# Second attention of a two-block transformer kernel: scaled keys, a negated row maximum, and output halves added by GpSimd

## The reference

```python
def attention_mixer(q, k, v, q_g, k_g, ang_row, ang_col):      # 8 query heads of 64, 2 key heads, 1024 tokens
    q = axial_rope(rmsnorm(q, q_g), ang_row, ang_col)
    k = axial_rope(rmsnorm(k, k_g), ang_row, ang_col)
    ...
    scale = HEAD_DIM ** -0.5                                    # 0.125
    def block(qblk):                                            # 128 queries
        s = jnp.einsum('bqkgd,bskd->bkgqs', qblk, k).astype(jnp.float32) * scale
        p = jax.nn.softmax(s, axis=-1)
        return jnp.einsum('bkgqs,bskd->bqkgd', p.astype(v.dtype), v)
```

## Time and profile before

| | |
|---|---|
| median of 3 runs | 2304.12 us (2303.63 to 2305.65) |
| span of the profiled execution | 2307.9 us |
| busy in the span: PE, DVE, ACT, POOL | 2218.0, 1617.7, 1089.5, 795.6 us |
| second attention | from 1357.5 us (first scores) to 1557.3 us (last values) |
| mean granted TensorE clock | 0.989 of full speed |

### The profile page before, as it was taken

The page is one execution under the profiler, slowest core; times in us unless marked ns, Lnnn a source line. Parts: engine busy times, 40 slices in busy tenths (PEclk is TensorE's granted clock), DMA queues, the critical chain, the costliest instruction groups (busy, mean ns, idle before and its releaser), DMA issues. The chain is left out here.

```text
span 2307.9 us, 29073 instructions
## 1 busy us (share of the span) xinstructions
PE 2218.0 (96%) x10136; PEld 1787.9 (77%) x10136; DVE 1617.7 (70%) x2247; ACT 1089.5 (47%) x1877; POOL 795.6 (34%) x579
## 2 busy tenths in 40 slices
PE   6999998999899999999998999999999999999998
PEld 4778887686678888888876767767778888887887
DVE  6468447626999999985797379994575555556686
ACT  5232256735644444455445368882343333334533
POOL 1030024513533232342023626661274444433310
PEclk9999999999999999999999999999999999999999
DMA  9156622033133333289944230003422333339986
GB/s 348 56 174 212 203 85 64 26 128 115 45 111 101 105 101 110 81 296 394 335 165 139 72 101 19 23 5 110 145 69 98 107 101 106 101 119 320 354 277 228
DMA packets 282565, 331.82 MB, mean 144 GB/s; under 512 B 18281, under 2 KB 180409, under 8 KB 282049
## 3 DMA queue, kind: packets, MB, share of 16 engines
q1 hardware_dynamic: 279760, 322.57, 41.4%
q0 software_dynamic: 2208, 7.37, 0.9%
q10 hardware_dynamic: 465, 0.17, 0.0%
HBM read 251.11 MB, written 78.94 MB: 143 GB/s over the span
## 5 line engine op out<-in xcount | busy, mean ns | idle before, releaser
L2643 PE MATMUL ps<-sum_hi,whi 128*128 128x512 f32 x640 | 249.5, 390 | 1.0 <-DVE wlo L2809 0.7
L2645 PE MATMUL ps<-sum_hi,wlo 128*128 128x512 f32 x640 | 249.0, 389 | 0.0
L2644 PE MATMUL ps<-sum_lo,whi 128*128 128x512 f32 x640 | 249.0, 389 | 0.0
L2669 PE MATMUL ps<-sum_lo,whi 128*128 128x512 f32 x616 | 240.7, 391 | 2.0 <-ACT arena L2754 2.0
L2671 PE MATMUL ps<-sum_lo,wlo 128*128 128x512 f32 x616 | 239.7, 389 | 0.0
L2670 PE MATMUL ps<-sum_lo,whi 128*128 128x512 f32 x616 | 239.7, 389 | 0.0
L2643 PE MATMUL ps<-hhi,whi 128*128 128x512 f32 x480 | 188.3, 392 | 9.0 <-DVE cbuf L3324 3.3
L226 DVE TENSOR_TENSOR wlo<-raw,whi 128x1024 fp32r<-128x1024 f32 x56 | 78.4, 1406 | 159.6 <-ACT whi L221 159.5
L2644 PE MATMUL ps<-hlo,whi 128*128 128x512 f32 x480 | 188.2, 392 | 0.0
L2645 PE MATMUL ps<-hhi,wlo 128*128 128x512 f32 x480 | 188.0, 392 | 0.0
L1732 POOL TENSOR_TENSOR cbuf<-cbuf,attn_stats 128x1024 f32<-128x1024 f32 x80 | 151.5, 1894 | 94.0 <-DVE attn_stats L1993 94.0
(11 more groups left out here) (450 smaller groups left out, 5575.2 us busy)
## 6 DMA issues: line engine op xcount, KB each, us to landing
shared<-ffn_blocks SPq DMA_DIRECT2D x154, 256.0 KB, 5.1
lead_work<-in_w_down SPq DMA_DIRECT2D x105, 256.0 KB, 4.4
arena<-in_w_down SPq DMA_DIRECT2D x100, 256.0 KB, 4.1
raw<-in_w_up SPq DMA_DIRECT2D x36, 512.0 KB, 5.1
ffn_blocks<-chunk_work SPq DMA_DIRECT2D x66, 256.0 KB, 2.3
ffn_blocks<-lead_work SPq DMA_DIRECT2D x66, 256.0 KB, 2.3
raw<-in_w_in SPq DMA_DIRECT2D x32, 512.0 KB, 4.7
arena<-in_w_ada SPq DMA_DIRECT2D x32, 512.0 KB, 5.5
```

Of the source, the lines that this page charges most:

```text
L2643: nc.tensor.matmul(o, hi[:, ws], mhi, start=fresh and k == 0, stop=False, skip_group_check=True)
L2644: nc.tensor.matmul(o, hi[:, ws], mlo, start=False, stop=False, skip_group_check=True)
L2645: mm = nc.tensor.matmul(o, lo[:, ws], mhi, start=False, stop=(k == 3), skip_group_check=True)
L2669: nc.tensor.matmul(o, hi[:, ws], mhi, start=fresh, stop=False, skip_group_check=True)
```

## The change

Four things are edited, all for the second attention alone. The keys are multiplied by 0.125 when they are split into high and low part, so the scores come out scaled and the exponential has no scale. The maximum is written with its sign turned by the reduction itself, and the small multiplication (L1977) is gone. ACT copies both halves of a group's output from PSUM, into `otmp` and a new `osum`. The two additions (old L2010) move from DVE's list to POOL's, behind the scaling of the closing unit, with a wait for ACT's copies ahead of them and a wait for their own end behind them.

```diff
-            otmp = cbuf[:, 2, 0:512]
+            otmp, osum = cbuf[:, 2, 0:512], cbuf[:, 2, 512:1024]
...
                     nc.scalar.activation(khh[64 * r:64 * r + 64, g, pad:kn], ka[64 * g:64 * g + 64, :],
-                                         ACT.Copy).then_inc(S["keys"], 1)
+                                         ACT.Copy, scale=SC if full else 1.0).then_inc(S["keys"], 1)
...
+                    if full:
+                        ins = nc.vector.scalar_tensor_tensor(out=klo[0:64, g, pad:kn], in0=k_, scalar=SC, in1=hi,
+                                                             op0=ALU.mult, op1=ALU.subtract)
...
+                    def outputs(n, gr, g):
+
+                        pool.wait_ge(S["out_copy"], gr.val(add=1))
+                        for half in range(2):
+                            o_, t_ = (v[0:64, :].rearrange("p (j s t) -> p j s t", s=2, t=P)[:, :, half, :] for v in (osum, otmp))
+                            ins = nc.gpsimd.tensor_tensor(qa[64 * half:64 * half + 64, 2 * g:2 * g + 2, tokens(n)],
+                                                          o_, t_, ALU.add)
+                        ins.then_inc(S["out"], 1)
+                        pool.wait_ge(S["out"], gr.val(add=1))
...
+                            gr = gr_closed(n, e)
+                            if gr is not None and full:
+                                outputs(n if e >= units else n + (-1), gr, 1 - e // units)
...
                     if full:
+                        outputs(At(NB - 1), group(At(NB - 1), per_n - 1), 1)
                         lead.pool_last(pool)
...
-                            nc.scalar.activation(prob[sl], up[sl][:, :], ACT.Exp, scale=SC, bias=st[:, sl, 4:5],
+                            nc.scalar.activation(prob[sl], up[sl][:, :], ACT.Exp, bias=st[:, sl, 4:5],
...
-                        nc.scalar.activation(otmp[0:64, :], ps_o[side(gr)][64:128, :], ACT.Copy).then_inc(S["out_copy"], 1)
+                        nc.scalar.activation(otmp[0:64, :], ps_o[side(gr)][64:128, :], ACT.Copy)
+                        nc.scalar.activation(osum[0:64, :], ps_o[side(gr)][0:64, :], ACT.Copy).then_inc(S["out_copy"], 1)
...
                         if full:
-                            nc.vector.tensor_scalar(ng, mx, -SC, None, ALU.mult).then_inc(S["neg_max"], 1)
+                            nc.vector.tensor_reduce(ng, up[sl].rearrange("p (r k) -> p r k", k=wk), AX.X, ALU.max,
+                                                    negate=True).then_inc(S["neg_max"], 1)
```

More of the change, by code:

```diff
@@ L1576, in attention @@
             per_n = 2 * units
-            names = ["keys", "klo", "zeros", "vturned", "vhi", "vlo", "scores", "stat", "neg_max", "exp", "recip", "scaled",
+            names = ["keys", "klo", "zeros", "vturned", "vhi", "vlo", "scores", "neg_max", "exp", "recip", "scaled",
                      "turned", "p_hi", "p_lo", "pv", "out"]
-            names += ["out_copy"] if full else ["sum", "band", "sinks", "sink_arg"]
+            names += ["out_copy"] if full else ["stat", "sum", "band", "sinks", "sink_arg"]
             S = {x: sem(f"{name}_{x}") for x in names}
@@ L1616, in dve_keys @@
                     dve.wait_ge(S["keys"], 2 * g + 2)
-                    nc.vector.tensor_tensor(klo[0:64, g, pad:kn], ka[64 * g:64 * g + 64, :],
-                                            khh[64 * g:64 * g + 64, g, pad:kn].bitcast(F32), ALU.subtract).then_inc(S["klo"], 1)
+                    k_, hi = ka[64 * g:64 * g + 64, :], khh[64 * g:64 * g + 64, g, pad:kn].bitcast(F32)
+                    if full:
+                        ins = nc.vector.scalar_tensor_tensor(out=klo[0:64, g, pad:kn], in0=k_, scalar=SC, in1=hi,
+                                                             op0=ALU.mult, op1=ALU.subtract)
+                    else:
+                        ins = nc.vector.tensor_tensor(klo[0:64, g, pad:kn], k_, hi, ALU.subtract)
+                    ins.then_inc(S["klo"], 1)
                 def dve_values(self, dve):
@@ L1972, in maxima @@
                         dve.wait_ge(S["scores"], u.val(add=1))
-                        nc.vector.tensor_reduce(mx, up[sl].rearrange("p (r k) -> p r k", k=wk), AX.X, ALU.max)\
-                          .then_inc(S["stat"], 1)
-                        dve.wait_ge(S["stat"], u.val(add=1))
                         if full:
-                            nc.vector.tensor_scalar(ng, mx, -SC, None, ALU.mult).then_inc(S["neg_max"], 1)
-                        else:
+                            nc.vector.tensor_reduce(ng, up[sl].rearrange("p (r k) -> p r k", k=wk), AX.X, ALU.max,
+                                                    negate=True).then_inc(S["neg_max"], 1)
+                        else:
+                            nc.vector.tensor_reduce(mx, up[sl].rearrange("p (r k) -> p r k", k=wk), AX.X, ALU.max)\
+                              .then_inc(S["stat"], 1)
+                            dve.wait_ge(S["stat"], u.val(add=1))
                             nc.vector.scalar_tensor_tensor(out=ng, in0=mx, scalar=-SC, in1=sink_neg[:, 4 * e:4 * e + 4],
@@ L2002, in split_probs @@
                               .then_inc(S["p_lo"], 1)
-                    def outputs(n, gr, g):
-                        dve.wait_ge(S["out_copy"], gr.val(add=1))
-                        for half in range(2):
-                            o_ = ps_o[side(gr)][0:64, :].rearrange("p (j s t) -> p j s t", s=2, t=P)[:, :, half, :]
-                            t_ = otmp[0:64, :].rearrange("p (j s t) -> p j s t", s=2, t=P)[:, :, half, :]
-                            ins = nc.vector.tensor_tensor(qa[64 * half:64 * half + 64, 2 * g:2 * g + 2, tokens(n)],
-                                                          o_, t_, ALU.add)
-                        ins.then_inc(S["out"], 1)
                     def ahead():
@@ L2042, in body @@
                                 mix.low(dve, 2)
-                            gr = gr_closed(n, e)
-                            if gr is not None and full:
-                                outputs(n if e >= units else n + (-1), gr, 1 - e // units)
                         if not more and full:
                             mix.dve_early(dve)
-                            outputs(n, group(n, per_n - 1), 1)
                     query_blocks(dve, ahead, body)
@@ L4013, in block_kernel @@
         retired = retire("attn_")
-        for x in ("keys", "klo", "zeros", "vturned", "vhi", "vlo", "scores", "stat", "neg_max", "exp", "recip", "scaled",
+        for x in ("keys", "klo", "zeros", "vturned", "vhi", "vlo", "scores", "neg_max", "exp", "recip", "scaled",
                   "turned", "p_hi", "p_lo", "pv", "out", "out_copy", "queries0_0", "queries0_1", "queries1_0", "queries1_1", "queries2_0", "queries2_1", "queries3_0", "queries3_1"):
```

## The result

| | before | after |
|---|---|---|
| median (lowest to highest), 4 runs each | 2304.89 us (2303.63 to 2308.24) | 2381.58 us (2381.11 to 2387.1) |
| ratio, 95% interval | | 1.0336 (1.0319 to 1.0352) |
| span of the profiled execution | 2307.9 us | 2379.7 us |
| busy: PE, DVE, ACT, POOL | 2218.0, 1617.7, 1089.5, 795.6 us | 2235.5, 1598.0, 1095.0, 820.6 us |
| mean granted TensorE clock | 0.989 | 0.979 |

A forecast was written before the change was run, and what follows sets the result against it. DVE and PE were both taken as full in the second attention, with PE's floor at 2.77 us a unit. Stops 51, clock 17 and end 3 us sum to +71 on the 2304.12 us median: 2375 us, range 2345 to 2398.

The forecast's parts named there:

- The chain: From a closing unit's transposes to the next transposes, through copies, additions and scaling: 7.17 us where 2.77 was.
- The stops: Behind 14 closing units PE waits for POOL's delayed scaling; a group takes 3.64 us longer, +51 us.
- The clock: After each of 14 stops PE runs some 3.5 us at half clock, costing 1.2 us each: +17 us (0 to 24).
- The end: `pool_last` stands behind the sixteenth group's additions and PE waits for it: +3 us (0 to 4).
- The spared DVE work: Removing L1977 in the second attention frees at most 10 us of DVE, counted at nothing since PE has no slack.
- ACT has the 0.5 us to spare: ACT's second copy adds 0.5 us at a closing unit, which ACT, busy 19.7 of 24 us, can spare.
- The clock that holds: Rival: the stops in the second attention come as worked out but cost no clock; 2358 us, chance 0.23.
- The clock low for twice as long: Rival: half clock behind each stop lasts over most of the next group's PE work; 2394 us, chance 0.13.
- The hidden stop: Rival: POOL's additions at closing units fit under PE's work and the kernel gets faster; 2293 us, chance 0.06.
- The likeliest case: The forecast itself, stops with lower clock and a delayed end: 2375 us, own range 2357 to 2389, chance 0.58.

The follow-up runs named there:

- the kernel whose PE is without a gap: Against the changed kernel: additions back on DVE with one ACT copy, copy and additions placed one group later; 2292.11 us, ratio 0.9944.
- the filled kernel: Changed kernel with 14 more matmuls of 512 columns ahead of each group's first transposes, keeping PE at work through the stop; 2361.24 us.
- the small additions: Changed kernel with POOL's two additions cut to 8 of 128 tokens each; 2383.36 us, ratio 1.0333.
- the tail in the other order: Changed kernel with `pool_last` put ahead of the last group's additions in POOL's list, with a wait for its end between; 2381.65 us.

## Why the prediction was right, step by step

**The mechanism holds.** POOL's list is in order, the additions wait in it for a chain that begins with the closing unit's transposes, and the scaling that PE needs is behind them. The move alone costs all; the same additions elsewhere in the list cost almost none of it.

**The chain, forecast 7.17 us from transposes to transposes.** It was 7.43 in the unit shown, where POOL needed 0.54 us between the additions and the scaling against 0.16 in most of them, so 7.05 in most. Copies 1.2 (1450.09 to 1451.28, forecast 1.1), hand-over 0.19 (0.3), pair 1.49 (1.5), scaling 1.9, as forecast. The addition is 0.717 us, as near to the line through L764 (0.95) as to a quarter of the scaling (0.47). No row showed this form, and 1.5 was picked between 0.95 and 1.9, so that this term fits to 0.01 is luck. The estimate of 0.56 us worked out from section 3.1 of the Trainium skill's GPSIMD Engine Reference was low; the measurement decides.

**The stops, forecast 14 x 3.64 = 51 us.** With the clock held by the filling matmuls the period is 15.37, which is 3.54 over that of before: 49.6 us.

**The clock, forecast 14 x 1.2 = 17 us.** It is 1.6 a stop, 22 us by the periods. I had put part of the low stretch into PE's idle time; the rows show it on the unit's work nearly whole in 13 of the 14 stops. This is the term that was mis-sized most, within its bounds of 0 and 1.75. The Trainium skill says in TensorE: Matmul & The Clock Gate, "HAM oscillation — how this bites in real kernels", that the drop comes back in every turn of the loop. The trace agrees: it does behind all 14.

**The end, forecast +3 us.** The loop carries 71.8, the whole 76.7, so about 5 are left for the tail, which is above the term's bounds of 0 and 4. The traces say the same: from the fifteenth group's additions to the end it is 754.4 us before and 759.0 after. The last additions took 1.6 us each instead of 0.72 and two of `pool_last`'s 128x8 instructions 1.07 and 1.06 instead of 0.20, both times with DVE's L3877 at work beside them; that is what I had not priced. Moving them does not win it back, since the stage behind then waits instead.

**The spared DVE work, forecast nothing.** In the changed kernel it is nothing (ratio 1.0336 with that work spared, 1.0334 with it done), but the reason given for it is wrong, and the result hid that. I read PE's floor as 2.77 us a unit from the earlier trace rows. It can be 2.71 (1459.91 to 1462.62 above); one pair of starts in a kernel where DVE paces PE is not PE's floor. That alone is little: the kernel whose PE is without a gap takes 11.00 us a group, not 4 x 2.71 = 10.85, and the forecast had 11.08. The larger mistake is that the prediction had found 0.76 us a group in which PE waits on DVE's work, and gave them to the additions, though L1977's 4 x 0.15 us are part of the same work. (They are also not in the fourth unit, as it says, but in the one behind it: 1444.56 to 1447.33 is the closing unit itself.) Without the move the kernel is 0.2% faster than before, and in the order that lets DVE's time count, L1977 is worth 11.3 us (0.9993 against 0.9944 of 2305). That is, within the intervals, all of the 64 x 0.15 = 10 us that the prediction gave as the most.

**ACT has the 0.5 us to spare.** Also wrong, and also hidden: it has them to spare in the sum, not at that place. One copy ahead of the next exponential costs 0.46 us a group.

**The rivals.** The clock that holds (2358) is what the filled kernel shows: 2361. The clock low for twice as long came behind one of the changed kernel's 14 stops and behind 11 of 14 with the small additions, where it cost 17.05 - 14.27 = 2.8 us a stop against 15.87 - 14.27 = 1.6 for the short one (14.27 is what most groups take with the clock held). The hidden stop fell with the first row of the waits.

**The range.** The likeliest case's own lower end is 2375 - 10 - 10 = 2355, not 2357.

## What to carry to other kernels

Before work is moved to an idle engine, write down what stands behind it in that engine's list and when its input arrives; an engine that is idle a third of the time (POOL in the earlier trace rows) stops the kernel if its one wait is ahead of something that the bound needs. Move the copy and the addition together to a point where their input is long there, here one group later. And measure each part of a change alone: a part that is worth 0.5% was invisible beside one that costs 3.4%, and in the old order it was worth less than half of that.

## What the runs showed that I had not expected

A shorter stop came with a longer time at half clock: stops of 3.2 us were mostly followed by 6.8 us at 0.50, stops of 4.2 us mostly by 3.4, and the time was the same. The length of the stop is not what decides, since both kinds occur behind stops of either length. What goes with it is the moment at which the clock fell. Over the 42 stops of three kernels (the changed one, only the additions moved, small additions) the low stretch was 6.8 us in the 16 cases where the clock fell 0.9 to 2.1 us before PE was at work again, and 3.4 us in the 26 where it fell at most 0.6 us before that, or after it. With the small additions it fell at 1419.61 for a restart at 1420.54, but at 1405.95 for one at 1404.67. Why the clock falls where it does stays open. That the clock is what ate the saving is shown, since with PE kept busy the saving came out in full.

POOL's instructions with two operands slow down beside DVE's with two operands in SBUF: 128x8 from 0.20 us to 1.06, and 64x256 from 0.72 to 1.6. No run took DVE's L3877 away, but the order of events differs between the kernels. In the kernel before, the 128x8 instructions of `pool_last` are over before that subtraction (there L3870) begins, and all four take 0.20. With the tail in the other order all of them but the last stand beside it (there L3878) and take 1.06; the last one starts 0.15 us after DVE is done and takes 0.20. It also goes the other way: in the changed kernel DVE's first L3877 took 1.71 us instead of 1.21 while POOL's addition at 1621.52 beside it kept its 0.74. And the two additions on DVE from two copies, 0.85 us in the loop, took 3.78 at 1556.63 beside POOL's instructions on 128x1008. The GPSIMD Engine Reference of the Trainium skill, section 8, says that GpSimd shares its SBUF interfaces with VectorE and contends with its instructions that have two inputs in SBUF; the trace agrees. Rows of the kernel before:

```profile
1552.94 0.20 POOL L3573 TENSOR_TENSOR small<-cbuf,pool_edges 128x8 f32<-128x8 f32 x1
...
1554.44 6.19 DVE L3870 TENSOR_TENSOR hlo<-arena,hhi 128x1024 fp32r<-128x1024 f32 x3
```

of the tail in the other order:

```profile
1621.23 7.95 DVE L3878 TENSOR_TENSOR hlo<-arena,hhi 128x1024 fp32r<-128x1024 f32 x5 [1.61 <-ACT hhi L3874]
...
1627.05 1.06 POOL L3582 TENSOR_TENSOR small<-cbuf,pool_edges 128x8 f32<-128x8 f32 x1
```

and DVE's of the changed kernel:

```profile
1621.63 6.80 DVE L3877 TENSOR_TENSOR hlo<-arena,hhi 128x1024 fp32r<-128x1024 f32 x5 [1.63 <-ACT hhi L3873]
1630.15 3.31 DVE L3877 TENSOR_TENSOR hlo<-arena,hhi 128x1024 fp32r<-128x1024 f32 x2 [1.72 <-ACT hhi L3873]
```
